# Half weight tiles as fillers of the attention stage, and the sliding attention run into its output projection

## The chip, the cores and the metric

One core of one Trainium2 chip runs the whole program. The metric is the time of one execution on the device in microseconds (us). The engines are TensorE (PE in the rows; PEld is its weight load), VectorE (DVE), ScalarE (ACT), GpSimd (POOL, all but unused) and SyncE (SP, which issues the loads of the weights).

## The reference

The input is one sequence of 256 tokens of width 1024, in f32. It goes through eight stages, each of which adds its result to the residual `x`: a gated feed-forward, a hybrid mixer, a cross-attention to a memory, a second gated feed-forward, an RWKV time mix, a feed-forward, a sliding-window attention with sinks, and a last feed-forward. Two of these hold the code that is changed.

```python
# the mixer: eight heads with three branches, eight forgetting heads
q_n, k_c, ..., gate_a, gate_b = split_cols(h @ w_in, IN_SPLITS)
y = sigmoid(gate_a) * (o_nsa @ w_up_nsa) + sigmoid(gate_b) * (o_fox @ w_up_fox)
return y @ w_out
# the sliding layer, 16 query heads on 2 shared key heads
m = max(max(s), sink);  p = exp(s - m)
p = p / (sum(p) + exp(sink - m))
return (p @ v) @ wo
```

## The kernel before

Activations are held transposed, 128 channels by 256 tokens. All large weights come as one stream of tiles, 128x2048 f32 (1 MB), through a ring of four places in SBUF. A product in f32 is made from three matmuls of rounded parts: each half of a tile (128x1024) is split by ScalarE, which copies a head (`tile_hi`, line 294), and by VectorE, which subtracts it from the original (`tile_lo`, line 304). There are four places for split halves, so a half can be split when the one four before it has been multiplied. `heads_after(done)` and `rests_after(done)` issue on ScalarE and on VectorE all the splits that are possible once `done` halves are multiplied, each with its waits; where such a call stands in an engine's program is where that engine stops for it. A half tile is 24 matmuls of 128x128 on 128x256 (`product`, lines 344 to 346).

`attention_stage` runs an attention as a pipeline of units. A unit is four lanes of 128 queries with 128 or 256 keys (for the second 128 queries). Each engine has its program as a loop over steps, in an order that is written out, and step `s` works on several units at once:

- TensorE: scores of unit `s` (after the maximum of unit `s-2`, whose banks it takes), a filler, transposes of the weights of unit `s-2` (line 979; after they are normed and the former transposes are copied away), values of unit `s-3`.
- VectorE: bias and scores together and their maximum (`combine`, then line 1043) for unit `s`, splits, the norming of unit `s-1` (lines 1054 to 1063), the store of the values of unit `s-3` as a pair (lines 338 and 339).
- ScalarE: four exponentials of unit `s` with their sums (line 1005), splits and the copy of the filler, the copy of the transposes of unit `s-2` (line 1022).

The mixer has twelve units: four with 128 keys and four with 256 from the three-branch heads, then two of each from the forgetting heads. Its fillers are the last four tiles of the gates' projection, a whole tile in each of steps 0 to 3, computed by `col_to_T` into bank 7 and copied to `gates_ab` by ScalarE. The next filler waits for that copy. The sliding attention has eight units (four with 128 keys, then four with 256) and no fillers; some steps of the query norm (`Last`) lie in its first steps. After step `ahead` (5 in the mixer, 2 in the sliding stage) one more half is split, so that the next stage finds its first two tiles split.

The block of either attention ends with a barrier of all engines. After the sliding attention `out_stage` multiplies its output by the four tiles `wo2` (`row_to_T`, into banks 4 to 7) and adds the result to `x` (`tail_vector`).

Of the kernel before, what the change touches and what calls it, by code (L numbers as in the profile page):

```python
# [363 lines left out]
def span(n, width):  # L364
    return slice(n * width, (n + 1) * width)
# [13 lines left out]
            between()  # L379


def col_to_natural(e, pe, g, src, bank):

    arrived(e, pe, g, 1)
    n = 2 * place_in_cut(g) % SPLIT
    w = tuple(part[:, n:n + 2, :].rearrange("p m (k n) -> p m k n", k=KC) for part in (e.w_hi, e.w_lo))
    for t in range(TT):
        for k in range(KC):
            mm = product(pe, e.ps[:, bank, span(t, 256)].rearrange("p (m n) -> p m n", m=2),
                         cut(src, ALL, k, span(t, P)), cut(w, ALL, ALL, k, ALL), k == 0, k == KC - 1)  # L390
    mm.then_inc(*e.tile_done.one(2))


def row_to_T(e, pe, g, src, k0, first, last):


    def chunk(w, k, m):
        return product(pe, e.ps[:, 4 + m // 2, span(m % 2, SEQ)], cut(w, ALL, span(m, P)), cut(src, ALL, k0 + k, ALL),
                       first and k == 0 and m % 2 == 0, last and k == 1 and m % 2 == 1)

    if last:
        halves = [arrived(e, pe, g, k) for k in range(2)]
        for m in range(KC):
            for k in range(2):
                mm = chunk(halves[k], k, m)
            if m % 2 == 1 and m < KC - 1:
                mm.then_inc(*e.sig("acc_ready").one())
        mm.then_inc(*e.tile_done.one(2))
        return
    for k in range(2):  # L410
        w = arrived(e, pe, g, k)
        for m in range(KC):
            mm = chunk(w, k, m)
        mm.then_inc(*e.tile_done.one())
# [69 lines left out]
    eng.wait_ge(*e.sig("residual_added").since(b + 1))  # L484


def add_to_residual(e, dve, b, scale, last_tile):

    if b < 3:
        dve.wait_ge(*e.sig("acc_ready").since(b + 1))  # L490
    else:
        multiplied(e, dve, last_tile)
    xs = e.x[:, two(b), :].rearrange("p m n -> p (m n)")
    if scale == 1.0:
        x = dve.tensor_tensor(xs, e.ps[:, 4 + b, :], xs, ALU.add)  # L495
    else:
        x = dve.scalar_tensor_tensor(out=xs, in0=e.ps[:, 4 + b, :], scalar=scale, in1=xs, op0=ALU.mult, op1=ALU.add)
    x.then_inc(*e.sig("residual_added").one())


# [6 lines left out]
    x.then_inc(*e.sig("x_ready").one())  # L507


def tail_vector(e, dve, scale, outs, last_tile):  # L510


    for n in range(6 if outs else 4):
        if n < 4:
            add_to_residual(e, dve, n, scale, last_tile)
# [393 lines left out]
    return n, slice(SEQ - n, SEQ)  # L909


def attention_stage(e, units, follows, fillers=(), hT=None, beside=None):

# [11 lines left out]
    last_tile = max([g for g, _ in fillers], default=-1)  # L925
    DEPTH = min(3, n)
    ahead = min(len(fillers) + 1, n - 1) + beside.delay

    with nc.Block() as block, ExitStack() as stack:
        tag = nc.next_id()  # L930
        sinks = any(unit.sink is not None for unit in units)
        s = e.sb(stack, f"scores{tag}", [P, DEPTH, 4, SEQ + (4 if sinks else 0)])
# [17 lines left out]
        @block.tensor  # L950
        def _(pe):
            for step in range(n + 3):
                if step < n:
                    if step >= 2:

                        pe.wait_ge(*max_ready.at(step - 1))
                    if beside:
                        beside.needed(pe, step)
                    b = 2 * (step % 2)
                    units[step].scores(pe, [e.ps[:, b + i, :].rearrange("p (l n) -> p l n", l=2)  # L960
                                            for i in range(2)]).then_inc(*scores_ready.one())
                if beside:
                    beside.tensor(pe, step)
                if step == len(fillers) and step >= 1:
                    pe.wait_ge(*filled.at(step))
                if step < len(fillers):
                    if step >= 1:
                        pe.wait_ge(*filled.at(step))
                    col_to_T(e, pe, fillers[step][0], hT, 7)
                u = step - 2  # L970
                if 0 <= u < n:
                    blocks = units[u].keys // P
                    pe.wait_ge(*weights_ready.at(u + 1))
                    if u >= 1:
                        pe.wait_ge(*copied.at(u))
                    for lane in range(4):
                        for kb in range(blocks):
                            at = (lane * blocks + kb) * P
                            tr = pe.transpose(e.ps[:, 4 + at // 512, at % 512:at % 512 + P],  # L979
                                              s[:, u % DEPTH, lane, kb * P:(kb + 1) * P], const(e, "ident"))  # L980
                    tr.then_inc(*turned.one())
                u = step - 3
                if 0 <= u < n:
                    pe.wait_ge(*copied.at(u + 1))
                    if u >= 1:

                        pe.wait_ge(*stored.at(u))
                    turned_weights = pT[:, u % 2, 0:4 * units[u].keys].rearrange(
                        "p (l b q) -> p l b q", l=4, q=P)


                    lasts = units[u].values(pe, turned_weights, out_ap(u))
                    for mm in lasts:
                        mm.then_inc(*values_ready.one(2 // len(lasts)))

        @block.scalar
        def _(act):
            for step in range(n + 2):
                if beside:
                    beside.first_scalar(act, step)  # L1000
                if step < n:
                    act.wait_ge(*max_ready.at(step + 1))
                    st = stat[:, step % 2]
                    for lane in range(4):
                        x = act.activation(summed(step)[:, lane], summed(step)[:, lane], ACT.Exp,  # L1005
                                           bias=st[:, 0, lane:lane + 1], accum_out=st[:, 1, lane:lane + 1])
                    x.then_inc(*sums_ready.one())
                if step < len(fillers):
                    g, dst = fillers[step]
                    tile_after(e, act, g)  # L1010
                    act.activation(dst, e.ps[:, 7, :], ACT.Copy).then_inc(*filled.one())
                if step == ahead:
                    heads_after(e, act, 2 * follows)
                u = step - 2
                if u >= 0:
                    act.wait_ge(*turned.at(u + 1))
                    if u >= 2:

                        act.wait_ge(*values_ready.at(2 * (u - 1)))
                    width = 4 * units[u].keys  # L1020
                    src = e.ps[:, 4:6, :].rearrange("p b n -> p (b n)")[:, 0:width]
                    act.activation(pT[:, u % 2, 0:width], src, ACT.Copy).then_inc(*copied.one())  # L1022

        @block.vector
        def _(dve):
            link = Chain(dve, dve_chain)
            for step in range(n + 3):
# [39 lines left out]
                if 0 <= u < n:  # L1067
                    dve.wait_ge(*values_ready.at(2 * (u + 1)))
                    units[u].store(link, out_ap(u)).then_inc(*stored.one())

def mixer_section(e):
    nc = e.nc
    with ExitStack() as stack:
# [22 lines left out]
        front = mixer_front(e, m)  # L1099
        attention_stage(e, [nsa_unit(e, m, t, i) for t in range(TT) for i in range(HPG)]  # L1100
                        + [fox_unit(e, m, t, j) for t in range(TT) for j in range(2)], FIRST["up"],
                        fillers=[(FIRST["gates"] + n - 1, m.ab[:, 2 * n + 2:2 * n + 4, :].rearrange("p m n -> p (m n)"))
                                 for n in range(FILLERS, 7)], hT=e.hT, beside=front)
# [1887 lines left out]
def swa_section(e, kvT):  # L2991
    with ExitStack() as stack:
# [9 lines left out]
        attention_stage(e, [swa_unit(e, s, t, j) for t in range(TT) for j in range(4)], FIRST["wo2"], beside=last)  # L3002
        out_stage(e, "wo2", s.o, [("ln_mlp1", e.hT)])


def swa_projections(e, s, kvT):
# [405 lines left out]
```

## Time and profile before

| | |
|---|---|
| median of three runs | 1501.92 us (1501.85 to 1503.39) |
| the profiled execution | 1512.18 us, its span 1510.9 us |
| TensorE matmul busy | 1420.5 us, 94% of the span |
| TensorE weight load busy | 1361.9 us, 90% |
| VectorE busy | 951.8 us, 63% |
| ScalarE busy | 713.4 us, 47% |
| mean granted clock of TensorE | 0.957 of full |

The span is the time from the first to the last instruction of the profiled execution; busy times of an engine are sums over its instructions. The weight loads and the matmuls of TensorE overlap each other. In rows of a timeline the first two numbers are the start and the length in us, and the bracket at the end says how long the engine was idle before and what released it; a row with a count (x4) is a series that follows without a gap, from the start of the first to the end of the last. The records of the matmuls are modelled at their ends: one lasts 0.28 us, but in a full series one starts every 0.12 us.

### The profile page before, as it was taken

The page shows a single profiled execution, that of the slowest core. Times are in us where ns is not written, and L with a number is a line of the kernel's source. Part 1 is how long each engine was busy: PE and PEld are TensorE (multiplying, and loading weights), DVE is VectorE, ACT ScalarE, POOL GpSimd, SP SyncE. Part 2 cuts the span into 40 slices and gives each one's busy share as a digit, 9 for nine tenths or more (in the row PEclk, how much of TensorE's full clock was granted, in tenths as well). Part 3 has the DMA queues.
Part 4 walks back from the last instruction along what each step waited for, and adds up shares of the span by engine and source line. Part 5 has one row for each costly group of instructions (what it writes and reads, how often), then busy time and mean ns, then how long its engine had stood idle before and what let it go on. Part 6 is the DMA issues. An engine that isn't in the chain of part 4 may idle for free. (4 is left out here: it accounts for less than half of the span.)

```text
span 1510.9 us, 28880 instructions
## 1 busy us (share of the span) xinstructions
PE 1420.5 (94%) x12748; PEld 1361.9 (90%) x12748; DVE 951.8 (63%) x1303; ACT 713.4 (47%) x1096; POOL 7.1 (0%) x12
## 2 busy tenths in 40 slices
PE   7999999997899999999989978998999996889999
PEld 7999999895799899999988977888999984889999
DVE  4655666468675456555678864566656678466565
ACT  5444454355464455444538423444444555454443
POOL 0000000000000000000000010000000000000000
PEclk9999999998999999999989986999999997999999
DMA  6555545640344334555514300023554530335542
GB/s 256 205 196 185 183 154 196 250 169 1 131 177 168 126 126 168 198 193 172 191 57 171 140 3 30 29 85 140 183 207 168 196 112 1 140 140 189 202 168 84
DMA packets 33108, 222.47 MB, mean 147 GB/s; under 512 B 3879, under 2 KB 5295, under 8 KB 6616
## 3 DMA queue, kind: packets, MB, share of 16 engines
q1 hardware_dynamic: 31928, 219.57, 40.3%
q8 instruction: 100, 1.64, 0.4%
q10 hardware_dynamic: 1056, 1.07, 0.2%
q14 instruction: 24, 0.20, 0.0%
HBM read 219.54 MB, written 1.07 MB: 146 GB/s over the span
## 5 line engine op out<-in xcount | busy, mean ns | idle before, releaser
L304 DVE TENSOR_TENSOR tile_lo<-ring,tile_hi 128x1024 fp32r<-128x1024 f32 x396 | 476.1, 1223 | 321.9 <-ACT tile_hi L294 321.2
L294 ACT ACTIVATE tile_hi<-ring 128x1024 fp32r<-128x1024 f32 x396 | 408.3, 1054 | 293.4 <-PE ps L346 289.3
L344 PE MATMUL ps<-hT_hi,tile_hi 128*128 128x256 f32 x1664 | 472.7, 284 | 10.1 <-DVE hidden_lo L753 7.6
L345 PE MATMUL ps<-hT_lo,tile_hi 128*128 128x256 f32 x1664 | 469.1, 282 | 0.0
L346 PE MATMUL ps<-hT_hi,tile_lo 128*128 128x256 f32 x1664 | 468.8, 282 | 0.0
L344 PEld LDWEIGHTS ps<-hT_hi,tile_hi 128*128 128x128 f32 x1664 | 316.0, 190 | 16.6 <-DVE hidden_lo L753 8.0
L346 PEld LDWEIGHTS ps<-hT_hi,tile_lo 128*128 128x128 f32 x1664 | 316.2, 190 | 0.0
L345 PEld LDWEIGHTS ps<-hT_lo,tile_hi 128*128 128x128 f32 x1664 | 315.9, 190 | 0.0
L344 PE MATMUL ps<-hidden_hi,tile_hi 128*128 128x256 f32 x864 | 241.5, 280 | 0.0
L346 PE MATMUL ps<-hidden_hi,tile_lo 128*128 128x256 f32 x864 | 241.5, 280 | 0.0
L345 PE MATMUL ps<-hidden_lo,tile_hi 128*128 128x256 f32 x864 | 241.5, 280 | 0.0
L346 PEld LDWEIGHTS ps<-hidden_hi,tile_lo 128*128 128x128 f32 x864 | 164.1, 190 | 0.0
L345 PEld LDWEIGHTS ps<-hidden_lo,tile_hi 128*128 128x128 f32 x864 | 162.9, 188 | 0.0
L344 PEld LDWEIGHTS ps<-hidden_hi,tile_hi 128*128 128x128 f32 x864 | 162.2, 188 | 0.0
L709 ACT ACTIVATE hidden_hi<-hidden_whole 128x512 fp32r<-128x512 f32 x54 | 34.1, 632 | 116.2 <-DVE hidden_whole L740 67.3
L753 DVE TENSOR_TENSOR hidden_lo<-hidden_whole,hidden_hi 128x512 fp32r<-128x512 f32 x54 | 37.4, 692 | 40.6 <-ACT hidden_hi L709 30.6
L1005 ACT ACTIVATE scores<-scores,lane_stats 128x128 f32<-128x128 f32 (+3 forms) x80 | 35.5, 445 | 47.0 <-DVE lane_stats L1043 46.9
L979 PEld LDWEIGHTS ps<-const_sb,scores 128*128 128x128 f32 x120 | 17.7, 178 | 33.7 <-issue 25.7
L979 PE MATMUL ps<-const_sb,scores 128*128 128x128 f32 x120 | 23.1, 346 | 26.5 <-ACT weightsT L1022 18.2
L746 DVE TENSOR_TENSOR hidden_whole<-gate,token_scale 128x512 f32<-128x512 f32 x32 | 22.2, 693 | 37.5 <-ACT gate L706 37.5
L706 ACT ACTIVATE gate<-ps 128x512 f32<-128x512 f32 x32 | 19.1, 597 | 47.6 <-PE ps L346 47.6
L344 PE MATMUL ps<-y_turned,tile_hi 128*128 128x256 f32 x128 | 36.2, 283 | 1.9 <-DVE tile_lo L304 1.9
(459 smaller groups left out, 2134.9 us busy)
## 6 DMA issues: line engine op xcount, KB each, us to landing
ring<-stream SPq DMA_DIRECT2D x204, 1024.0 KB, 4.8
x_sb<-x SPq DMA_DIRECT2D x4, 256.0 KB, 4.1
bias<-f_dram ACTq DMA_DIRECT2D x1, 1024.0 KB, 8.2
fox_bias<-forget_dram SPq DMA_DIRECT2D x1, 1024.0 KB, 6.2
squares<-mem SPq DMA_DIRECT2D x1, 1024.0 KB, 4.8
out<-x_sb SPq DMA_DIRECT2D x4, 256.0 KB, 2.2
const_sb<-const SPq DMA_DIRECT2D x1, 577.0 KB, 9.6
small_sb<-small SPq DMA_DIRECT2D x1, 493.5 KB, 9.7
```

The lines of the kernel that those rows point to most:

```text
L294: act.activation(e.w_hi[:, n % SPLIT, :], e.ring[:, tile % RING, span(n % 2, HALF)], ACT.Copy).then_inc(e.tile_hi.handle, 1)
L304: dve.tensor_tensor(e.w_lo[:, n % SPLIT, :], e.ring[:, CUT[n // 2] % RING, span(n % 2, HALF)], e.w_hi[:, n % SPLIT, :].bitcast(F32), ALU.s ...
L344: pe.matmul(out, left[0], right[0], start=start, stop=False)
L345: pe.matmul(out, left[0], right[1], start=False, stop=False)
L346: return pe.matmul(out, left[1], right[0], start=False, stop=stop)
L706: act.activation(tmp[:, j % 2, :], e.ps[:, 2 * (j % 2), :], ACT.Relu).then_inc(*act_done.one())
L709: act.activation(slot(hid[0], j), whole[:, j % 2, :], ACT.Copy).then_inc(*hi_ready.one())
L746: link.done(dve.tensor_tensor(halves_of(both), halves_of(tmp[:, j % 2, :]), scale_pairs(e), ALU.mult))
L753: dve.tensor_tensor(slot(hid[1], j), both, slot(hid[0], j).bitcast(F32), ALU.subtract).then_inc(*hidden_ready.one())
L979: tr = pe.transpose(e.ps[:, 4 + at // 512, at % 512:at % 512 + P], s[:, u % DEPTH, lane, kb * P:(kb + 1) * P], const(e, "ident"))
L1005: x = act.activation(summed(step)[:, lane], summed(step)[:, lane], ACT.Exp, bias=st[:, 0, lane:lane + 1], accum_out=st[:, 1, lane:lane + 1])
```

## The change

In the mixer the four fillers become eight, one half tile in each of steps 0 to 7 (`half_col_to_T`, with its own copy of 128x256 on ScalarE). On TensorE the filler is moved from before the transposes to the end of the step. On ScalarE the step begins with the copy of the filler of the step before, then the copy of the transposes, then the splits, and then the exponentials. On VectorE the splits are moved from before the norming to the end of the step. Step `ahead` of the mixer is now 9; in the sliding stage it stays 2. Both attentions get the new order.

The sliding attention no longer ends with a barrier. In its last three steps (8 to 10) TensorE takes one half tile of `wo2` each, into banks 0 to 3, as soon as the units are stored whose channels it needs; `swa_output` does the other three halves and the last tile, and takes the place of `out_stage`.

```diff
@@ the new products
+def half_col_to_T(e, pe, g, half, src, bank):
+    w = chunks_of(arrived(e, pe, g, half))
+    for k in range(KC):
+        mm = product(pe, e.ps[:, bank, span(half, SEQ)], cut(w, ALL, k, ALL), cut(src, ALL, k, ALL), k == 0, k == KC - 1)
+    mm.then_inc(*e.tile_done.one())
-def row_to_T(e, pe, g, src, k0, first, last):
+def row_to_T(e, pe, g, src, k0, first, last, bank=4):
...
@@ attention_stage, TensorE
-    with nc.Block() as block, ExitStack() as stack:
+    stored.mark()
+    with (Open(nc) if tail else nc.Block()) as block, ExitStack() as stack:
...
-                if step == len(fillers) and step >= 1:
-                    pe.wait_ge(*filled.at(step))
-                if step < len(fillers):
-                    if step >= 1:
-                        pe.wait_ge(*filled.at(step))
-                    col_to_T(e, pe, fillers[step][0], hT, 7)
                 u = step - 2
...
+                if tail and step >= n:
+                    if step == n:
+                        pe.wait_ge(*max_ready.at(n))
+                    tail.tensor(pe, step - n)
+                if step == len(fillers) and step >= 1:
+                    pe.wait_ge(*filled.at(step))
+                if step < len(fillers):
+                    if step >= 1:
+                        pe.wait_ge(*filled.at(step))
+                    g, half, _ = fillers[step]
+                    half_col_to_T(e, pe, g, half, hT, 7)
@@ attention_stage, ScalarE (the copy of the transposes, unchanged, now stands between these two)
+                if 1 <= step <= len(fillers):
+                    g, half, dst = fillers[step - 1]
+                    multiplied(e, act, g, half)
+                    act.activation(dst, e.ps[:, 7, span(half, SEQ)], ACT.Copy).then_inc(*filled.one())
...
+                if step < len(fillers):
+                    g, half, dst = fillers[step]
+                    heads_after(e, act, 2 * g + half)
+                if step == ahead:
+                    heads_after(e, act, 2 * follows)
                 if step < n:
                     act.wait_ge(*max_ready.at(step + 1))
...
-                if step < len(fillers):
-                    g, dst = fillers[step]
-                    tile_after(e, act, g)
-                    act.activation(dst, e.ps[:, 7, :], ACT.Copy).then_inc(*filled.one())
-                if step == ahead:
-                    heads_after(e, act, 2 * follows)
@@ attention_stage, VectorE
-                if step < len(fillers):
-                    rests_before(e, dve, fillers[step][0] + 1)
-                if step == ahead:
-                    rests_after(e, dve, 2 * follows)
                 u = step - 1
...
                     units[u].store(link, out_ap(u)).then_inc(*stored.one())
+                if step == ahead:
+                    rests_after(e, dve, 2 * follows)
+                if step < len(fillers):
+                    rests_after(e, dve, 2 * fillers[step][0] + fillers[step][1])
@@ the sliding section
-        out_stage(e, "wo2", s.o, [("ln_mlp1", e.hT)])
+        swa_output(e, s)
+class SlidingOutput:
+    def half_tile(self, pe, i, k):
+        e = self.e
+        pe.wait_ge(*self.stored.since(5 + i))
+        w = arrived(e, pe, FIRST["wo2"] + i, k)
+        for m in range(KC):
+            mm = product(pe, e.ps[:, m // 2, span(m % 2, SEQ)], cut(w, ALL, span(m, P)), cut(self.o, ALL, 2 * i + k, ALL),
+                         i == 0 and k == 0 and m % 2 == 0, False)
+        mm.then_inc(*e.tile_done.one())
+    def tensor(self, pe, n):
+        self.half_tile(pe, n // 2, n % 2)
+def swa_output(e, s):
...
+            for n in range(3, 6):
+                rest.tensor(pe, n)
+            pe.wait_ge(*stored.since(8))
+            row_to_T(e, pe, g0 + 3, s.o, 6, False, True, 0)
...
+            heads_after(e, act, 2 * (g0 + 3))
+            tail_scalar(e, act, outs, then=lambda: heads_after(e, act, 2 * (g0 + 4)))
...
+            rests_after(e, dve, 2 * (g0 + 3))
+            tail_vector(e, dve, 1.0, outs, g0 + 3, 0)
+            rests_after(e, dve, 2 * (g0 + 4))
```

## Rows read from the trace of the kernel before

**Rows 1.** The page, part 1: busy us, share of the span, instructions.

```profile
PE 1420.5 (94%) x12748; PEld 1361.9 (90%) x12748; DVE 951.8 (63%) x1303; ACT 713.4 (47%) x1096; POOL 7.1 (0%) x12
```

**Rows 2.** Stretch, length; busy us (PE, PEld, DVE, ACT, POOL); granted clock, DMA share, GB/s.

```profile
313.00:340.00 27.00, 26.92 (x234) 25.69 (x234) 16.04 (x32) 15.59 (x44) 0.00 (x0) 1.00 0.42 151
353.00:360.00 7.00, 3.69 (x22) 2.70 (x22) 6.22 (x16) 1.75 (x5) 0.00 (x0) 0.50 0.00 1
315.10:380.80 65.70, 53.34 (x460) 43.62 (x459) 48.60 (x120) 36.05 (x109) 0.00 (x0) 0.90 0.14 49
380.80:392.80 12.00, 7.00 (x58) 5.60 (x56) 5.90 (x19) 4.60 (x11) 0.00 (x0) 0.72 0.01 1
1257.30:1295.10 37.80, 24.13 (x180) 17.74 (x180) 27.70 (x83) 17.80 (x55) 0.00 (x0) 0.75 0.00 1
1295.30:1318.50 23.20, 23.14 (x192) 23.09 (x192) 9.88 (x11) 8.60 (x12) 0.00 (x0) 1.00 0.61 214
```

**Rows 3.** Waits, 315.1 to 380.8: us in total, times, longest us.

```profile
ACT scores L1005 <- DVE lane_stats L1043: 28.8, 11, 5.3
DVE tile_lo L304 <- ACT tile_hi L294: 13.8, 5, 3.1
```

**Rows 4.** Timeline of TensorE in the mixer's attention.

```profile
312.75 0.71 PE L1530 MATMUL ps<-k_sel_win,queries 64*128 64x128 f32 x8
...
320.04 0.39 PE L344 MATMUL ps<-hT_hi,tile_hi 128*128 128x256 f32 x1
...
325.94 0.72 PE L1530 MATMUL ps<-k_sel_win,queries 64*128 64x128 f32 x8
...
343.44 0.63 PE L979 MATMUL ps<-const_sb,scores 128*128 128x128 f32 x4 [1.48 <-DVE scores L1063]
...
344.96 1.13 PE L1530 MATMUL ps<-k_sel_win,queries 64*128 64x256 f32 x8
...
365.74 0.71 PE L1575 MATMUL ps<-squares,queries 64*128 64x128 f32 x8
367.72 1.06 PE L979 MATMUL ps<-const_sb,scores 128*128 128x128 f32 x8 [1.26 <-ACT weightsT L1022]
...
370.10 0.71 PE L1575 MATMUL ps<-squares,queries 64*128 64x128 f32 x8
...
383.59 1.94 PE L979 MATMUL ps<-const_sb,scores 128*128 128x128 f32 x8 [2.75 <-ACT weightsT L1022]
```

**Rows 5.** Timeline of VectorE in the mixer's attention.

```profile
332.16 2.36 DVE L304 TENSOR_TENSOR tile_lo<-ring,tile_hi 128x1024 fp32r<-128x1024 f32 x2 [2.67 <-ACT tile_hi L294]
...
366.50 0.76 DVE L1581 TENSOR_TENSOR scores<-ps,cmp_in 128x256 f32<-128x256 f32 x2
...
380.97 1.14 DVE L1063 TENSOR_SCALAR scores<-scores,lane_stats 128x256 f32<-128x256 f32 x4
...
392.31 0.42 DVE L339 TENSOR_TENSOR o_parts<-ps,o_parts 128x256 fp32r<-128x256 f32 x1
```

**Rows 6.** Timeline of ScalarE in the mixer's attention.

```profile
318.18 1.04 ACT L294 ACTIVATE tile_hi<-ring 128x1024 fp32r<-128x1024 f32 x1
```

**Rows 7.** ScalarE by shape, 1195 to 1300: count, busy us, mean ns.

```profile
L3033 ACT ACTIVATE q_swa<-ps 128x256 f32<-128x256 f32 x1 | 0.4, 378 | 0.0
```

**Rows 8.** Timeline of VectorE in the sliding attention.

```profile
1259.38 1.23 DVE L304 TENSOR_TENSOR tile_lo<-ring,tile_hi 128x1024 fp32r<-128x1024 f32 x1 [2.02 <-ACT tile_hi L294]
...
1265.83 0.17 DVE L1039 COPY scores<-sinks_sb 128x4 f32<-128x4 f32 x1 [0.86 <-PE ps L3206]
...
1282.99 1.14 DVE L1063 TENSOR_SCALAR scores<-scores,lane_stats 128x256 f32<-128x256 f32 x4
```

**Rows 9.** Timeline of TensorE at the sliding attention's end.

```profile
1286.04 1.91 PE L979 MATMUL ps<-const_sb,scores 128*128 128x128 f32 x8 [3.06 <-ACT weightsT L1022]
...
1293.02 1.09 PE L3224 MATMUL ps<-weightsT,v_swa 128*64 128x128 f32 x16 [1.07 <-DVE o_swa_lo L339]
1295.36 0.36 PE L344 MATMUL ps<-o_swa_hi,tile_hi 128*128 128x256 f32 x1 [1.25 <-PEq L929]
```

More of the change, by code:

```diff
@@ L391, in col_to_natural @@
     mm.then_inc(*e.tile_done.one(2))
-def row_to_T(e, pe, g, src, k0, first, last):
+def row_to_T(e, pe, g, src, k0, first, last, bank=4):
     def chunk(w, k, m):
-        return product(pe, e.ps[:, 4 + m // 2, span(m % 2, SEQ)], cut(w, ALL, span(m, P)), cut(src, ALL, k0 + k, ALL),
+        return product(pe, e.ps[:, bank + m // 2, span(m % 2, SEQ)], cut(w, ALL, span(m, P)), cut(src, ALL, k0 + k, ALL),
                        first and k == 0 and m % 2 == 0, last and k == 1 and m % 2 == 1)
@@ L484, in wait_for_added, with add_to_residual @@
     eng.wait_ge(*e.sig("residual_added").since(b + 1))
[L487 removed]
+def add_to_residual(e, dve, b, scale, last_tile, bank=4):
     if b < 3:
@@ L494, in add_to_residual @@
     if scale == 1.0:
-        x = dve.tensor_tensor(xs, e.ps[:, 4 + b, :], xs, ALU.add)
+        x = dve.tensor_tensor(xs, e.ps[:, bank + b, :], xs, ALU.add)
     else:
-        x = dve.scalar_tensor_tensor(out=xs, in0=e.ps[:, 4 + b, :], scalar=scale, in1=xs, op0=ALU.mult, op1=ALU.add)
+        x = dve.scalar_tensor_tensor(out=xs, in0=e.ps[:, bank + b, :], scalar=scale, in1=xs, op0=ALU.mult, op1=ALU.add)
     x.then_inc(*e.sig("residual_added").one())
@@ L909, in keys_of, with attention_stage @@
     return n, slice(SEQ - n, SEQ)
-def attention_stage(e, units, follows, fillers=(), hT=None, beside=None):
+def attention_stage(e, units, follows, fillers=(), hT=None, beside=None, tail=None):
     e.stage()
@@ L924, in attention_stage @@
          "values_ready", "values_stored", "filler_copied", "dve_step"))
-    last_tile = max([g for g, _ in fillers], default=-1)
+    last_tile = max([g for g, _, _ in fillers], default=-1)
     DEPTH = min(3, n)
     ahead = min(len(fillers) + 1, n - 1) + beside.delay
-    with nc.Block() as block, ExitStack() as stack:
+    stored.mark()
+    with (Open(nc) if tail else nc.Block()) as block, ExitStack() as stack:
         tag = nc.next_id()
@@ L1000, in _ @@
                     beside.first_scalar(act, step)
[L1001 to L1007, printed above, removed]
-                if step < len(fillers):
-                    g, dst = fillers[step]
-                    tile_after(e, act, g)
-                    act.activation(dst, e.ps[:, 7, :], ACT.Copy).then_inc(*filled.one())
-                if step == ahead:
-                    heads_after(e, act, 2 * follows)
+                if 1 <= step <= len(fillers):
+                    g, half, dst = fillers[step - 1]
+                    multiplied(e, act, g, half)
+                    act.activation(dst, e.ps[:, 7, span(half, SEQ)], ACT.Copy).then_inc(*filled.one())
                 u = step - 2
@@ L1022, in _ @@
                     act.activation(pT[:, u % 2, 0:width], src, ACT.Copy).then_inc(*copied.one())
+                if step < len(fillers):
[3 more added lines that the diff above has]
+                    heads_after(e, act, 2 * follows)
+                if step < n:
+                    act.wait_ge(*max_ready.at(step + 1))
+                    st = stat[:, step % 2]
+                    for lane in range(4):
+                        x = act.activation(summed(step)[:, lane], summed(step)[:, lane], ACT.Exp,
+                                           bias=st[:, 0, lane:lane + 1], accum_out=st[:, 1, lane:lane + 1])
+                    x.then_inc(*sums_ready.one())
         @block.vector
@@ L1101, in mixer_section @@
                         + [fox_unit(e, m, t, j) for t in range(TT) for j in range(2)], FIRST["up"],
-                        fillers=[(FIRST["gates"] + n - 1, m.ab[:, 2 * n + 2:2 * n + 4, :].rearrange("p m n -> p (m n)"))
-                                 for n in range(FILLERS, 7)], hT=e.hT, beside=front)
+                        fillers=[(FIRST["gates"] + n - 1, half, m.ab[:, 2 * n + 2 + half, :])
+                                 for n in range(FILLERS, 7) for half in range(2)], hT=e.hT, beside=front)
         memory.raw, memory.sq = e.sq, queries
@@ L3001, in swa_section, with __init__, _ @@
         last = swa_projections(e, s, kvT)
-        attention_stage(e, [swa_unit(e, s, t, j) for t in range(TT) for j in range(4)], FIRST["wo2"], beside=last)
-        out_stage(e, "wo2", s.o, [("ln_mlp1", e.hT)])
+        attention_stage(e, [swa_unit(e, s, t, j) for t in range(TT) for j in range(4)], FIRST["wo2"], beside=last, tail=SlidingOutput(e, s))
+        swa_output(e, s)
+class SlidingOutput:
+    def __init__(self, e, s):
+        self.e, self.o, self.stored = e, s.o, e.sig("values_stored")
+    def half_tile(self, pe, i, k):
[9 more added lines that the diff above has]
+def swa_output(e, s):
+    e.stage()
+    g0 = FIRST["wo2"]
+    outs = [("ln_mlp1", e.hT)]
+    stored = e.sig("values_stored")
+    rest = SlidingOutput(e, s)
+    with Open(e.nc) as block:
+        @block.sync
+        def _(sp):
+            feed(e, sp, g0 + 4)
+        @block.tensor
+        def _(pe):
+            mark_tail(e)
+            for n in range(3, 6):
+                rest.tensor(pe, n)
+            pe.wait_ge(*stored.since(8))
+            row_to_T(e, pe, g0 + 3, s.o, 6, False, True, 0)
+        @block.scalar
+        def _(act):
+            heads_after(e, act, 2 * (g0 + 3))
+            tail_scalar(e, act, outs, then=lambda: heads_after(e, act, 2 * (g0 + 4)))
+        @block.vector
+        def _(dve):
+            rests_after(e, dve, 2 * (g0 + 3))
+            tail_vector(e, dve, 1.0, outs, g0 + 3, 0)
+            rests_after(e, dve, 2 * (g0 + 4))
 def swa_projections(e, s, kvT):
```

4 lines of the change are left out of this document (2 added, 2 removed).

## The prediction

> **What bounds the kernel now.** I read the page first: TensorE is busy 94% of the span [rows 1], so most stages run at its pace, and only stretches where it stands can give time. Then the busy time by stretch, around the two attentions. From the mixer's first `combine` to its last maximum (315.1 to 380.8) TensorE has 53.34 us of 65.7 and VectorE 48.60: neither is full [rows 2]. In 313 to 340, with the whole tiles, TensorE is full (26.92 of 27.00) and VectorE has 16.04; from 353 to 360 it is the other way round, 3.69 of 7.00 against 6.22, and TensorE's clock is granted at 0.50, which is its 1.2 GHz level [rows 2]. So the tiles stand where VectorE has time and are gone where TensorE has. The waits say what sets the pace of the first steps: VectorE waited 13.8 us for `tile_hi`, in five waits, and ScalarE 28.8 us for maxima [rows 3]. A step of it goes around: maximum, four exponentials, two heads, and only then VectorE's two rests (it waited 2.67 us for the first) [rows 5], behind which stands the norming, and behind that the next `combine`. In the sliding stage TensorE is busy for 24.13 of 37.80 us at a mean clock of 0.75, and then `wo2` runs alone, 23.20 us with TensorE full [rows 2].
>
> **The mixer: steps 0 to 7, TensorE's queue.** A step of the new order is, on TensorE, scores, transposes, values, half tile; on VectorE, `combine`, maximum, norming, store, one rest; on ScalarE a half copy, the transposes' copy, one head, exponentials. Nothing that circulates is as long as before, since no head stands between a maximum's exponentials and the norming. I add up TensorE's queue from its rows.
> - Half tile: the whole tile takes 5.90 (320.04 to 325.94) [rows 4], so 2.95, and eight are 23.6.
> - Scores: 0.75 with 128 keys, 1.13 with 256 [rows 4]; four of each are 7.5.
> - Transposes and values together: 1.52 (343.44 to 344.96) with 128 keys, 2.38 (367.72 to 370.10) with 256 [rows 4]. In steps up to 7 there are five of both (units 0 to 4) and transposes alone of unit 5: 4 x 1.52 + 2.38 + 1.0 = 9.5.
> - Sum 40.6. To it comes one wait: the half tile of step 1 needs the first copy, which stands behind the exponentials of unit 0. These end at 318.18 [rows 6], and a copy of 128x256 takes 0.38 [rows 7], so to 318.6; TensorE would be there at 312.75 + 0.75 + 2.95 + 0.75 = 317.2, counted from the stage's first scores [rows 4]. That is 1.4.
>
> So scores of unit 8 start at about 312.75 + 42.0 = 354.8, where they started at 365.74 [rows 4]: 10.9 us earlier. Both other engines fit below it. For a step with 256 keys TensorE's sum is 1.13 + 2.38 + 2.95 = 6.5; VectorE's is about 5.7 (2.5 for `combine` and maximum, 1.5 for the norming, 0.6 for the store, 1.15 for a rest, estimated from half of the 2.36 of two [rows 5] and from the spacing of its steps), ScalarE's 4.4.
>
> **Steps 8 to 11, and the end.** Here there are no fillers in either kernel and VectorE is the pace: `combine` of unit 8 to the last maximum took 366.50 to 380.85 (the norming at 380.97 follows it) [rows 5]. The new kernel has one rest more here (1.15), because step `ahead` is 9, and loses short waits of about as much; I keep 14.4. The last maximum is then at 354.8 + 0.75 + 14.4 = 370.0. Behind it, before: the exponentials of unit 11, then the copy of unit 9's transposes, then unit 10's transposes at 383.59, which waited 2.75 for that copy [rows 4], though its norming was over at 380.97 + 1.14 = 382.1 [rows 5]. With the copy ahead of the exponentials, transposes start there: 1.4 less of the 11.9 from the last maximum to the last store (392.31 + 0.42 [rows 5]). The clock was 0.72 in this stretch [rows 2], and I leave it so. The end is 370.0 + 10.5 = 380.5 against 392.7: **12.2 us less**. The barrier and `up_stage` come behind it unchanged.
>
> A rule bears on which queue to add up. In this stretch matmuls are busy 81% and weight loads 66%, VectorE 74% [rows 2]. The Trainium skill, "Perfetto Trace Analysis", Identifying the Most-Contended Engine, says that matmul busy share misleads, and that the weight loads' share tells TensorE's headroom. By it VectorE is the fullest engine, and the mixer should come near VectorE's own sum; what that gives is the second case below. I go by the starts of the series in rows 4, which are no busy share.
>
> **The sliding stage, steps 2 to 7.** VectorE waited 2.02 us for the head and did its rest before the norming of unit 1 [rows 8]. Now the norming (1.0) goes into that wait, and the head comes some 0.6 earlier, since it no longer follows the exponentials: 1.6 less. Earlier transposes also free the scores of unit 4, for which VectorE waited 0.86 [rows 8]. Together 2.5. The transposes' copy ahead of the exponentials costs nothing here: exponentials that start up to 1 us later are still done before VectorE has taken the next unit's `combine` and maximum.
>
> **Its end, joined to `wo2`.** Before, unit 6's transposes began at 1286.04, after 3.06 of waiting for a copy that stood behind exponentials [rows 9]; its norming was over at 1282.99 + 1.14 = 1284.1 [rows 8]. With the 2.5 before it this is 1281.6 in the new kernel. From there I take TensorE's queue without a wait: two groups of transposes and three of values at 1.09 [rows 9], and eight halves at 23.20 / 8 = 2.9 [rows 2], 28.7 in all. Between values of units 6 and 7 lies a half tile, which covers the copy and store that cost 1.07 and the barrier's 1.25 [rows 9]. The first half needs the store of unit 4 only; half 4 needs a split that follows the last transposes' copy and the last store, about 3 us before its turn. To this comes the clock: the first group ran 1.91 for 1.09 [rows 9]; two such groups are +1.6. The end of `wo2` is 1281.6 + 28.7 + 1.6 = 1311.9 against 1318.5 [rows 2]: **6.6 us less**. What cannot be read is how the half tiles run if the clock is low when they come: at the lower level a half takes up to 2.9 more, and no row shows one. The bounds are 0 for none, 8.7 for all three; I take 0, since unit 6's own groups stand ahead of them.
>
> SyncE is no longer stopped by the barrier and issues the loads of the next tiles inside the attention, where the DMA share is 0.00 [rows 2]; no row waits there for a load. The banks 0 to 3 are free after the last maximum, and the next stage's first product waits for `x` anyway.
>
> **Sum.** 12.2 + 6.6 = 18.8 us of 1512.18 in the profiled execution. The median of the runs is 1501.92, 0.68% less; in that measure it is 18.7, and the time **1483.2 us**.
>
> **The rivals.**
> 1. *VectorE's sum, not TensorE's, is the pace of the mixer's first steps.* Its 48.60 of 65.7 [rows 2] leave 17.1 to lose; some 1 us of starting waits stays. Then the mixer gives 16.1 + 1.4 = 17.5 instead of 12.2, and the kernel 1478. Against it: TensorE's queue is in order, and its steps come to 6.5 against 5.7.
> 2. *The clock falls inside the new work.* Transposes, values and scores are slower by about 0.9 per group at the lower level [rows 9], a half by up to 2.9. Two steps of the mixer (2 x 5.3) at that level, or the three halves at the sliding end (8.7), give some 9 back: 1492. For it: 0.50 in 353 to 360 and 0.72 at the end, in stretches that TensorE half fills [rows 2]. Against: with whole tiles it was 1.00, and in my sum TensorE idles 1.4 us in 42.
> 3. *Slower than before: the mixer's eight filler steps run at 1.2 GHz.* The price is 5.3 a step (2.95 for the half, 2.4 for the rest), the point of decision is between three and four steps, where 18.8 us are spent; all eight give 42.4 less the 18.8, so 1525. It needs waits of TensorE in every step, for instance for the copy behind exponentials; I see one, in step 1.
> 4. *The joined end does nothing:* the half tiles only fill TensorE's waits while the last steps stretch by as much, since transposes now queue behind a half (2.9). Then the sliding end gives only the 2.5 and the 1.9 from 1284.1 to 1286.04, and the time is 1485. In my sum TensorE is full from 1281.6 on, so a queue there is no loss.
>
> **How the numbers follow.** The forecast 0.60, with 1479 to 1488 as its own range; rival 1 0.13; rival 2 0.14; rival 4 0.07; rival 3 0.03, of which a third with so few slow steps that nothing is left to see; other 0.03, as likely above as below 1502. The range reaches to rivals 1 and 2: 1475 to 1492. A measurement of this kernel can tell 0.2% (3 us) from no change. Faster 0.95, same 0.02, slower 0.03.
>
> **What the profile after will show.** Eight series of 24 matmuls, each after values, with scores following at once; unit 8's scores near 354.8, the last store of the mixer near 380.5; VectorE's waits for `tile_hi` gone from the stretch (13.8 to under 2); the granted clock 1.00 to about 350. In the sliding stage the unit 6 transposes near 1281.6 less the mixer's 12.2, three halves of `wo2` between them and the last values, and no gap of 1.25. I am wrong if steps 4 to 7 are not 6 to 6.5 us apart, if the clock shows 0.50 among the halves, or if `up_stage` or the last feed-forward takes longer than before.

## The result and the profile after

The changed kernel takes 1482.04 us in the median of four runs (1478.27 to 1485.44), the kernel before 1501.88: ratio 0.9871, 95% interval 0.9849 to 0.9892. Run again beside the experiments it gave 1483.8 (six runs) against 1503.8, 0.9868 [0.9843, 0.9892]. The forecast was 1483.2.

The profiled execution took 1483.38 us, span 1482.1. That is 28.8 us below the profiled one of before, 9 more than the medians say. The trace shows where it lies. Counted inside each stage, the mixer's attention went from 77.60 to 64.96 us (first `combine` to last store), and the sliding stage from 70.94 to 63.65 (from where its first `combine` starts to where the last addition to `x` starts): 12.64 + 7.29 = 19.9, and the medians differ by 19.8. The other 8.9 us are in code that is the same in both: 2.3 ahead of the mixer's attention, 3.1 between the two stages, 3.5 behind the sliding stage. The last section shows how far executions of one kernel differ there; why they do stays open.

The busy time by stretch of the changed kernel, as in [rows 2]: the same two stretches of the mixer, then first `combine` to last maximum, last maximum to last store, and the sliding stage's later part.

```profile
313.00:340.00 27.00, 25.57 (x225) 22.05 (x225) 22.61 (x59) 19.10 (x63) 0.00 (x0) 1.00 0.34 117
353.00:360.00 7.00, 7.00 (x79) 5.34 (x76) 6.55 (x22) 5.22 (x16) 0.00 (x0) 1.00 0.00 0
312.86:367.04 54.18, 49.78 (x460) 41.16 (x458) 48.30 (x119) 37.19 (x114) 0.00 (x0) 1.00 0.17 59
367.04:377.90 10.86, 7.19 (x56) 5.71 (x56) 5.94 (x19) 4.12 (x10) 0.00 (x0) 0.69 0.01 2
1239.30:1276.90 37.60, 30.77 (x237) 24.50 (x238) 27.58 (x84) 20.64 (x59) 0.00 (x0) 0.80 0.08 29
```

The third row is the change in one line. VectorE does the same 48.3 us, TensorE the same series at the full clock (49.78 for 53.34), and the stretch is 54.18 us instead of 65.70: both are now nearly full (92% and 89%), at a granted clock of 1.00 where the mean was 0.90.

The waits of the changed kernel in that stretch (engine and line, released by; us, times, longest) answer to [rows 3].

```profile
ACT weightsT L1027 <- PE ps L982: 9.3, 8, 1.7
ACT scores L1037 <- DVE lane_stats L1060: 5.5, 4, 2.7
DVE scores L1553 <- PE ps L1547: 4.1, 6, 1.3
```

VectorE's 13.8 us of waiting for `tile_hi` are gone. What it waits for now is TensorE's scores, 4.1 us in the steps with fillers, which points to TensorE's queue as the pace. Its timeline, as in [rows 4]:

```profile
310.48 0.71 PE L1547 MATMUL ps<-k_sel_win,queries 64*128 64x128 f32 x8
...
316.31 0.38 PE L344 MATMUL ps<-hT_hi,tile_hi 128*128 128x256 f32 x1 [1.43 <-ACT gates_ab L1018]
...
328.56 1.14 PE L1547 MATMUL ps<-k_sel_win,queries 64*128 64x256 f32 x8
...
334.21 1.13 PE L1547 MATMUL ps<-k_sel_win,queries 64*128 64x256 f32 x8
...
339.87 1.13 PE L1547 MATMUL ps<-k_sel_win,queries 64*128 64x256 f32 x8
...
345.92 1.14 PE L1547 MATMUL ps<-k_sel_win,queries 64*128 64x256 f32 x8
346.99 1.09 PE L982 MATMUL ps<-const_sb,scores 128*128 128x128 f32 x8
348.01 1.09 PE L1563 MATMUL ps<-weightsT,v_sel_win 128*64 128x128 f32 x16
349.03 0.43 PE L1565 MATMUL ps<-cmp_weightsT,cmp_v 15*64 15x128 f32 x4
349.40 0.39 PE L344 MATMUL ps<-hT_hi,tile_hi 128*128 128x256 f32 x1
...
352.45 0.71 PE L1592 MATMUL ps<-squares,queries 64*128 64x128 f32 x8
...
364.21 0.66 PE L982 MATMUL ps<-const_sb,scores 128*128 128x128 f32 x4 [1.43 <-DVE scores L1076]
364.83 0.66 PE L1608 MATMUL ps<-weightsT,squares 128*64 128x128 f32 x8
368.45 1.97 PE L982 MATMUL ps<-const_sb,scores 128*128 128x128 f32 x8 [2.96 <-DVE scores L1076]
```

From 345.92 to 352.45 is one full step with 256 keys, without a gap: scores, transposes, values, half tile, and scores again, 6.53 us. The three steps before it (4, 5 and 6) start their scores at 328.56, 334.21 and 339.87 and take 5.65, 5.65 and 6.05 us: their scores have 256 keys, but some or all of their transposes and values are of units with 128. The scores of unit 8 stand 352.45 - 310.48 = 41.97 us behind those of unit 0, where they stood 365.74 - 312.75 = 52.99 [rows 4].

TensorE at the joined end, as in [rows 9], and VectorE's rest of the sliding stage, as in [rows 8]:

```profile
1263.22 1.09 PE L982 MATMUL ps<-const_sb,scores 128*128 128x128 f32 x8 [2.59 <-DVE scores L1076]
1264.24 1.63 PE L3293 MATMUL ps<-weightsT,v_swa 128*64 128x128 f32 x16
1265.80 0.58 PE L344 MATMUL ps<-o_swa_hi,tile_hi 128*128 128x256 f32 x1
...
1269.75 1.04 PE L982 MATMUL ps<-const_sb,scores 128*128 128x128 f32 x8
1270.72 1.09 PE L3293 MATMUL ps<-weightsT,v_swa 128*64 128x128 f32 x16
...
1274.81 1.09 PE L3293 MATMUL ps<-weightsT,v_swa 128*64 128x128 f32 x16
```

```profile
1240.81 1.23 DVE L304 TENSOR_TENSOR tile_lo<-ring,tile_hi 128x1024 fp32r<-128x1024 f32 x1 [0.42 <-ACT tile_hi L294]
```

Unit 6's transposes wait for their norming and no longer for a copy; behind them TensorE has no gap. The first half tile took 3.95 us (1265.80 to 1269.75), not 2.9: its first dozen of 24 matmuls ran at the lower clock (0.50 from 1265.80 to 1268.00, 1.00 behind that).

### The profile page after: what moved, and what is told of

It reads as the page before. It is cut to its first block and busy times, and to the rows that moved or that the text cites. A ratio compares the mean times of both kernels' runs of the same rounds, so it can differ in the third digit from the quotient of the medians.

```text
span 1482.1 us, 28884 instructions
## 1 busy us (share of the span) xinstructions
PE 1408.5 (95%) x12748; PEld 1351.0 (91%) x12748; DVE 951.4 (64%) x1303; ACT 714.4 (48%) x1100; POOL 7.1 (0%) x12
## 5 line engine op out<-in xcount | busy, mean ns | idle before, releaser
L346 PE MATMUL ps<-hidden_hi,tile_lo 128*128 128x256 f32 x864 | 238.5, 276 | 0.0
L709 ACT ACTIVATE gate<-gate 128x512 f32<-128x512 f32 x22 | 13.9, 632 | 46.8 <-DVE gate L742 46.8
L346 PE MATMUL ps<-y_turned,tile_lo 128*128 128x256 f32 x128 | 35.8, 280 | 0.0
```

The costliest lines, as they stand in the source:

```text
L346: return pe.matmul(out, left[1], right[0], start=False, stop=stop)
```

## The experiments

My theory was that of the prediction: in the mixer's filler steps TensorE's queue is the pace once the heads and rests are out of the circle, and both the order and the halving are needed for that. All stage times below are read from the traces as above; the runs' medians spread by about 1%, so ratios decide only between large steps.

| kernel | ratio to before [95%] | mixer us | sliding us |
|---|---|---|---|
| before | 1 | 77.60 | 70.94 |
| changed | 0.9871 [0.9849, 0.9892] | 64.96 | 63.65 |
| changed, again | 0.9868 [0.9843, 0.9892] | 65.26 | 62.11 |
| e1 mixer only | 0.9930 [0.9897, 0.9962] | 64.75 | 70.68 |
| e2 sliding only | 0.9933 [0.9906, 0.9960] | 77.81 | 62.11 |
| e3 whole tiles, new order | 0.9985 [0.9961, 1.0009] | 72.31 | 70.84 |
| e4 halves, old order | 1.0076 [1.0047, 1.0105] | 87.57 | 70.64 |
| e5 copy behind exponentials | 0.9847 [0.9815, 0.9878] | 67.11 | 66.94 |
| e6 rests before norming | 0.9875 [0.9840, 0.9911] | 65.62 | 65.49 |
| e7 short halves | 0.9866 [0.9835, 0.9897] | 63.27 | 62.14 |
| e8 no halves between | 0.9857 [0.9828, 0.9886] | 64.69 | 64.65 |
| i1 last half late | 0.9837 [0.9804, 0.9870] | 61.53 | 63.69 |
| i1, again | 0.9850 [0.9823, 0.9877] | 61.55 | 63.67 |

**The two parts alone.**

```diff
# e1: attention_before and out_stage for the sliding layer;  e2: attention_before with whole tiles for the mixer
-        attention_stage(e, [swa_unit(...)], FIRST["wo2"], beside=last, tail=SlidingOutput(e, s))
-        swa_output(e, s)
+        attention_before(e, [swa_unit(...)], FIRST["wo2"], beside=last)
+        out_stage(e, "wo2", s.o, [("ln_mlp1", e.hT)])
```

> The mixer's attention is as in the changed kernel, the sliding attention and its output stage are as in the kernel before. If the two parts are independent and the mixer gives what the traces show (77.6 us from the first combine to the last store before, 64.96 after), the time is 12.6 us below the kernel before, 1489.3. If the mixer gives less and something of the sliding part carried the gain, it is above 1493.

> The sliding attention and its output are as in the changed kernel, the mixer is as before. Independent parts: 7.3 us below the kernel before (the traces of before and after, from the first combine of the stage to the last addition to x: 70.9 and 63.7), 1494.6. If joining gives only the barrier and the order nothing: under 2 us below.

In the stages both came out as expected, 64.75 and 62.11 us, each with the other part as before; the two ratios multiply to 0.986. The ratios that were expected, 0.992 and 0.995, lie within the intervals of e1 and e2. The parts are independent, as far as the stage times show.

**Order and halving apart.**

```diff
# e3, to e1 (ScalarE and VectorE then copy and split for a whole tile in a step)
-                    half_col_to_T(e, pe, g, half, hT, 7)
+                    col_to_T(e, pe, fillers[step][0], hT, 7)
...
# e4, to e1: on TensorE the filler before the transposes; on ScalarE
+                (exponentials of the step)
                 heads_after(e, act, 2 * g + half); multiplied(e, act, g, half); (copy of the half)
                 (copy of the transposes)
-                (exponentials of the step)
# and on VectorE rests_after(...) before the norming
```

> e1 with whole tiles again: four fillers in steps 0 to 3, but in the new order (filler last on TensorE, copies and heads ahead of the exponentials, rests last on VectorE). Theory A (order and halving both count, TensorE's queue is the pace while it has fillers, VectorE's after them): TensorE needs 6.65, 8.1, 7.2 and 8.2 us for steps 0 to 3, then four steps at VectorE's 4.5, so the scores of unit 8 start 49 us after those of unit 0 (before 53.0, after 42.0); with 1.4 at the end the time is 5 us below the kernel before, 1497. Theory B (the order alone is what matters): 42 and 1489. Theory C (halving alone matters): 53 and 1500.5.

> e1 with the eight half tiles in steps 0 to 7, but in the old order (filler before the transposes, exponentials before heads and copies, rests before the norming). Theory A: the circle maximum, exponentials, head, rest, norming, store, combine is the pace in all eight steps, 6.3 to 6.9 us with 128 keys and 8.6 with 256; the scores of unit 8 start 58 to 60 us after those of unit 0, and the time is 5 to 7 us above the kernel before. Theory C (halving alone matters): 42 and 1490.

Whole tiles in the new order give 5.3 us in the stage, as theory A has it; in the runs e3 can't be told from the kernel before. The scores of unit 8 stand 48.7 us behind those of unit 0, for 49, but in part by luck: the four steps with tiles took 28.1 us, for 30.2, and the four after them 20.5, for 18. Halves in the old order cost 10.0 us, 1.0076 in the runs: halving alone makes the kernel slower. I had said 5 to 7. Up to `combine` of unit 8 it is 5.4 us more (56.74 for 51.37 behind that of unit 0; its scores stood at 54.4, not at 58 to 60), and behind it 4.6 more, which I had left out: 3.3 of these are in step 9, where the wait for the next stage's split now stands. VectorE in e4, one step of the circle, and two of its waits from 311 to 372:

```profile
352.23 1.22 DVE L1058 TENSOR_REDUCE lane_stats<-scores 128x4 f32<-128x1024 f32 x1
356.54 1.23 DVE L304 TENSOR_TENSOR tile_lo<-ring,tile_hi 128x1024 fp32r<-128x1024 f32 x1 [3.09 <-ACT tile_hi L294]
357.68 0.17 DVE L1069 RECIPROCAL lane_stats<-lane_stats 128x4 f32<-128x4 f32 x1
...
360.98 1.22 DVE L1058 TENSOR_REDUCE lane_stats<-scores 128x4 f32<-128x1024 f32 x1
```

```profile
DVE tile_lo L304 <- ACT tile_hi L294: 20.3, 7, 3.1
DVE scores L1713 <- PE ps L1707: 0.6, 1, 0.6
```

Maximum to maximum is 8.75 us, with 3.09 of waiting for a head that stands behind four exponentials. For TensorE's scores VectorE waits only 0.6 us in all, so the filler's old place on TensorE isn't what holds this circle up. Eight halves meet that wait in seven steps, four whole tiles in four.

**Which queue is the pace.**

```diff
# e7: a part of the gates' projection is not computed
-    for k in range(KC):
+    for k in range(KC - 2):
```

> The changed kernel with the last two of eight chunks left out of each half filler in the mixer (18 matmuls instead of 24, so that part of the gates' projection isn't computed): 0.73 us less on TensorE in each of steps 0 to 7, nothing else. TensorE's queue alone as the pace: combine of unit 8 comes 5 us earlier, at 35 behind that of unit 0 (40.35). VectorE's sum as the pace (rival 1 of the prediction): nothing changes. My sum of both queues says VectorE's floor (5.4 to 5.6 in steps with 256 keys) is met after part of it: 37, and 3 us less in all.

With 5.8 us less on TensorE the mixer lost 1.7 (64.96 to 63.27), and `combine` of unit 8 came at 38.39 behind that of unit 0 instead of 40.35. Steps 4 to 7 are then 5.31, 5.57, 5.58 and 5.57 us long, with VectorE full:

```profile
342.60 1.28 DVE L1553 TENSOR_TENSOR scores<-ps,bias 128x512 f32<-128x512 f32 x2
...
347.05 1.22 DVE L304 TENSOR_TENSOR tile_lo<-ring,tile_hi 128x1024 fp32r<-128x1024 f32 x1
348.18 1.28 DVE L1553 TENSOR_TENSOR scores<-ps,bias 128x512 f32<-128x512 f32 x2
```

In the changed kernel the same steps of VectorE are 5.66, 5.65, 6.05 and 6.11 us long. So TensorE's queue is the pace there, and VectorE's floor lies 0.1 us below it in steps 4 and 5 and 0.5 in steps 6 and 7. Combine of unit 8 came 2.0 us earlier, less than the 3 I expected; TensorE, done sooner, waited 2.15 us for the first copy instead of 1.43, and step 1 took 6.34 us for 5.14: in this execution the clock fell behind that wait.

```profile
318.82 0.38 PE L344 MATMUL ps<-hT_hi,tile_hi 128*128 128x256 f32 x1 [2.15 <-ACT gates_ab L1018]
...
321.80 1.23 PE L1547 MATMUL ps<-k_sel_win,queries 64*128 64x128 f32 x8
```

**Single places undone.**

```diff
# e5, ScalarE in both attentions:      (copy of the transposes) moved behind (exponentials)
# e6, VectorE in both attentions:      rests_after(...) moved before the norming
# e8: nothing between the last steps of the sliding attention
-                    tail.tensor(pe, step - n)
-            for n in range(3, 6):
+            for n in range(6):
```

> The changed kernel with one thing undone in both attentions: ScalarE copies the transposes behind the exponentials of the step again. My theory: nothing in the mixer's steps 0 to 7, where TensorE's queue is the pace and the copy has slack; 1.1 to 1.4 us more from the last maximum to the last store of the mixer (10.77 in the changed kernel) and about 2 more at the sliding stage's end, 3 to 4 us in all. Rival: the place of the copy is worth nothing by itself and the 1.2 us seen there came from the granted clock: 0.

> The changed kernel with one thing undone: VectorE takes the rest before the norming again, while everything else stays, the head ahead of the exponentials too. My theory: the rest waits for a head that stands behind the copy of the transposes, and the norming behind both; 0.5 us more in a step with 128 keys, 0.9 with 256, so combine of unit 8 at 45 instead of 40.35 us behind that of unit 0, and about 1.5 more in the sliding stage: 6 us in all. Rival: with the head ahead of the exponentials VectorE's place for the rest no longer matters, and the time is that of the changed kernel within 1 us.

> The changed kernel with one thing undone: no half tile of wo2 stands in the last three steps of the sliding attention; all of wo2 follows behind the last values, still without a barrier. If the halves fill waits of TensorE that remain (the copy and the store between the last groups, some 3 us beside the barrier), the end comes 2 to 3 us later than in the changed kernel (63.65 us from the first combine to the last addition to x). Rival 4 of the prediction (the halves only stretch the last steps): no later. Most of the 7.3 us then came from the removed barrier and the order.

With the copy behind the exponentials the mixer takes 2.2 us more. In the steps with fillers it costs nothing, as expected (`combine` of unit 8 at 40.47 for 40.35); behind the last maximum it costs 1.1, as expected, and from unit 8 to the last maximum 1.0 (14.8 for 13.8), which I hadn't foreseen. The sliding stage takes 3.3 us more (4.8 against the second execution of the changed kernel), but the copy's place can't have all of it. TensorE's groups at the end ran at the lower clock for longer than in the changed kernel:

```profile
1266.59 1.94 PE L982 MATMUL ps<-const_sb,scores 128*128 128x128 f32 x8 [1.44 <-ACT weightsT L1039]
...
1270.37 0.58 PE L344 MATMUL ps<-o_swa_hi,tile_hi 128*128 128x256 f32 x1
...
1274.39 1.03 PE L982 MATMUL ps<-const_sb,scores 128*128 128x128 f32 x8
```

I estimate from the lengths of two groups of transposes, two of values and the half tile that the low clock cost about 4 us there, for 1.6 in the changed kernel; that leaves some 1 us of the 3.3 for the order itself. Whether the order brought the longer stretch at the low clock, by the waits of 2.67 and 1.44 us ahead of the transposes, one execution doesn't show.

With the rests before the norming `combine` of unit 8 comes only 0.7 us later (41.09 for 40.35), where I had said 4.7: in the steps with fillers I was wrong, and the rival right. VectorE in e6 waits only 0.4 for the head, because the head already stands ahead of the exponentials, and rest, norming and store still fit into TensorE's 6.1 us:

```profile
352.07 1.22 DVE L1060 TENSOR_REDUCE lane_stats<-scores 128x4 f32<-128x1024 f32 x1
353.68 1.23 DVE L304 TENSOR_TENSOR tile_lo<-ring,tile_hi 128x1024 fp32r<-128x1024 f32 x1 [0.39 <-ACT tile_hi L294]
```

But the mixer's total, 65.62 us, hides what comes behind. From unit 8 to the last maximum e6 takes 1.8 us more (15.6 for 13.8; in step 9 VectorE waits 1.28 for the head), and the end, from there to the last store, 1.9 less, because the clock was back at its upper level for the last transposes (1.09 and 1.06 us, for 1.97 and 1.94 in the changed kernel):

```profile
356.80:372.51 15.71, 12.41 (x116) 9.04 (x115) 13.73 (x37) 9.33 (x29) 0.00 (x0) 0.89 0.00 1
372.51:381.33 8.82, 4.86 (x56) 3.86 (x56) 5.75 (x18) 4.13 (x10) 0.00 (x0) 1.00 0.00 0
```

Up to the last maximum the rests' place is thus worth 2.5 us in this execution, some of it the lower clock (0.89 for 1.00). In the sliding stage it is worth 2.0 up to the norming of unit 6 (35.40 for 33.40 behind the first `combine`), a little more than the 1.5 I had said. Of e4's loss, then, the head behind the exponentials is the larger part: e4 differs from e6 also in the place of the copies and of the filler, but e5 and e4's waits show these to be small in the steps with fillers. The head's place was not undone alone.

The halves between the last sliding steps are worth 1.0 us (64.65 against 63.65), or 2.5 against the second execution (62.11). The first is the fairer comparison: e8 lost about 1.6 us to the low clock in its last groups (estimated from their lengths), as the first execution did, and the second lost nothing there. That is less than the 2 to 3 I expected. The rest of the 7.3 us is 3.0 up to the norming of unit 6 (36.40 to 33.40 behind the first `combine`) and some 3.3 for the copy's place and the barrier, which no run takes apart. In runs none of these three can be told from the changed kernel.

**A better version.**

```diff
# i1: halves in steps 0 to 6 and 11, the next stage's split in step 12 (every loop then asks at_step)
-    ahead = min(len(fillers) + 1, n - 1) + beside.delay
+    ahead = 12 if fillers else 1 + beside.delay
+    at_step = {p: i for i, p in enumerate([0, 1, 2, 3, 4, 5, 6, 11])} if fillers else {}
...
```

> A version that may be better: the half tiles stand in steps 0 to 6 and the eighth in step 11, where TensorE waited 2.96 us for the last norming; the half of the next stage is split in step 12 instead of 9. If a half fits the wait: 0.5 us less in step 7, 1.1 less on VectorE in step 9, and the granted clock stays up in the last two groups of transposes (1.9 instead of 1.1 each), 2 to 3 us less than the changed kernel in all. If the half only delays the last transposes by what it takes, 0.

The mixer takes 61.53 us, 3.4 less than the changed kernel: 1.7 by step 7, where I had said 0.5 (`combine` of unit 8 at 38.70 for 40.35), 0.8 from there to the last maximum and 0.9 behind it. The half fits the wait of 2.96, and the last transposes take 1.09 each where they took 1.97 and 1.94; the clock is granted at 1.00 in the last stretch instead of 0.69:

```profile
365.48 0.39 PE L344 MATMUL ps<-hT_hi,tile_hi 128*128 128x256 f32 x1
...
368.51 1.09 PE L983 MATMUL ps<-const_sb,scores 128*128 128x128 f32 x8
...
371.70 1.09 PE L983 MATMUL ps<-const_sb,scores 128*128 128x128 f32 x8 [1.51 <-DVE scores L1078]
```

```profile
367.12:377.00 9.88, 6.28 (x69) 5.11 (x67) 8.01 (x21) 5.34 (x12) 0.00 (x0) 1.00 0.00 0
```

Both kernels once more, side by side:

> The changed kernel once more, beside the others on one chip: 0.985 to 0.99 of the kernel before. The mixer's attention again within 0.2 us of 64.96 from first combine to last store; the sliding stage 62.1 or 63.7, after the clock in its first half tile.

> The version with the eighth half in step 11, again: its mixer attention took 61.53 us against 64.96, so 3.4 us or 0.23% below the changed kernel in this same call.

The mixer's time repeated to 0.3 us for the changed kernel (I had said 0.2; the difference is behind the last maximum) and to 0.02 for i1. The changed kernel's sliding stage took 62.11 us for 63.65, one of the two values I had named. The medians are 1483.8 and 1481.74, 0.14% apart for 0.23%, in the expected direction, but the intervals of the ratios overlap: the gain of i1 over the changed kernel is shown in the stage's time; in the whole kernel's time it is not.

## Why the prediction was right

The time, 1482.04 us, is 1.2 below the forecast, and the two attentions gave what the terms said, by the mechanism named: with head and rest out of the circle, TensorE's queue became the pace.

- **Steps 0 to 7.** Forecast 42.0 us from scores 0 to scores 8, measured 41.97. Its parts stood too: the wait of step 1 was 1.43 for 1.4, a full step with 256 keys 6.53 for 6.5. But the prediction also named 6 to 6.5 us for each of steps 4 to 7, or else it would be wrong, and two of the four lie outside: 5.65, 5.65, 6.05 and 6.53. The sum had counted the transposes and values of steps 4 and 5 with 128 keys, the sign and the comparison with VectorE (6.5 against 5.7) had not.
- **Steps 8 to 11.** Kept at 14.4, measured 13.84 (before 14.27). The added rest was covered: VectorE is busy 13.45 us of it, for 12.66 before. That the earlier transposes did this is shown by e5, where the same steps take 14.8.
- **From the last maximum.** 10.5 forecast, 10.77 measured, with the clock as low as before (0.69 for 0.72). Undoing the copy's place alone made it 11.82 at the same clock (0.71), so the mechanism named is the right one. This miss and the one above it, of 0.3 and 0.6 us, have opposite signs. The mixer as a whole gave 12.6 for 12.2.
- **Sliding, up to the last normings.** 2.5 forecast, 3.0 measured.
- **The joined end.** 4.1 of the 6.6 were to come here; 4.3 came in the profiled execution and 5.8 in the second. The +1.6 for the clock was placed on the groups of transposes and values; 0.5 fell on one group of values and 1.05 on the first half tile. The sum came out by luck: the first term was too large, and I had taken 0 for the half tile, within bounds of 0 to 8.7. In the second execution nothing ran low there and the end was 1.5 us sooner.
- **The other signs of being wrong.** The clock did show 0.50 in one half tile, at the joined end. `up_stage` and the projection behind it did not take longer: from the mixer's last store to the first addition to `x` it is 45.1 us in both. From the sliding stage's last addition to the end, the last feed-forward above all, it is 188.0 us for 191.5, in code that is the same.
- **The rivals.** 1 (VectorE's sum) fell: it gave 17.5 us for the mixer, where 12.6 were measured, and in e7 less work on TensorE shortened the steps. But it fell by little, since VectorE's floor is 0.1 to 0.5 us a step below. 2 (the clock) happened once, in the sliding stage, for 1.6 us, and in e7. 3 did not happen. 4 holds in part: e8 shows that two thirds or more of the sliding gain need no half tile in between.
- **The fullest engine.** The weight loads are busy for 76% of the new stretch and VectorE for 89%, and yet e7 shows TensorE's queue as the pace, above a floor of VectorE close below. The Trainium skill, "Perfetto Trace Analysis", Identifying the Most-Contended Engine, judges TensorE's headroom by its MFU and by the weight loads' busy share. By that share VectorE would again have been named, so here measurement and page differ; the MFU was not worked out.

## What to carry to other kernels

Where an engine in order serves both a circle of dependent steps and work that can wait, ask for each item whether it stands inside the circle; take it out first, and only then cut it finer. Cut finer alone, it is a wait in more steps (e4: 10 us lost in the stage). Then add up each engine's queue for one step from the starts of its series, and put what is left over where the fullest engine waits, which may be in the drain at the end. When one place is undone to price it, compare the granted clock too: in e5 and e6 it changed with the edit and moved the stage's time by 2 us either way.

## What the runs showed of the hardware

Executions of one kernel differ by about 1%, though the granted clock is 1.00 in stretches like the two below. The busy time of TensorE in two dense stretches that no edit touches, for the kernel before and for the changed one:

```profile
60.00:270.00 210.00, 209.75 (x1744) 1.00 0.53 187
1390.00:1430.00 40.00, 40.00 (x341) 1.00 0.47 163
```

```profile
60.00:270.00 210.00, 209.70 (x1769) 1.00 0.54 192
1390.00:1430.00 40.00, 40.00 (x349) 1.00 0.57 207
```

The same series has 1744 or 1769 matmuls in 210 us, and 341 or 349 in 40 us: 117 against 115 ns each in the second stretch. Both profiles hold 12748 matmuls in all, so no missing records make the difference. All thirteen profiles have one of these two paces there (341 or 342, and 348 to 350), and one can be slow in the first stretch and fast in the second. The stretch between the two attentions was 847.68 and 855.56 us in two executions of i1. What sets the pace stays open, and these two stretches account only for a part of the 8.9 us. Such differences are why two profiles of 1510.9 and 1482.1 us must not be subtracted, and why the stages were measured each from its own first instruction.
